# Forget-gate sums added as a spread bias, 64-row score matmuls side by side, and a vector of ones set on the chip

## What is computed

```python
x = x + 0.5 * swiglu(rms_norm(x), ffn1)
p = rms_norm(x) @ w_in        # FoX q, k, v, f; HGRN2 q, f, i, g; S5 u
x = x + concat(fox(p), hgrn2(p), s5(p)) @ w_out
x = x + 0.5 * swiglu(rms_norm(x), ffn2)
```

```python
c = cumsum(log_sigmoid(f_logit), axis=1)            # one row of 256 sums per head
for qs, qe in ((0, 128), (128, 256)):
    s = einsum('bhqd,bhkd->bhqk', q[:, :, qs:qe], k[:, :, :qe]) * scale
    s = s + c[:, :, qs:qe, None] - c[:, :, None, :qe]
    p = softmax(where(mask, s, -inf))
    out = einsum('bhqk,bhkd->bhqd', p, v[:, :, :qe])
```

## Time and profile before

| | |
|---|---|
| median of 3 runs | 1018.65 us (1017.72 to 1018.83) |
| the profiled execution | 1019.28 us |
| its span, first to last instruction | 1017.5 us |
| granted TensorE clock over the span | 1.000 |
| PE busy | 1008.7 us (99%) |
| DVE, ACT, POOL busy | 734.4, 559.8, 225.8 us |
| mean transfer rate | 175 GB/s |

### The profile page before, as it was taken

The page is one execution under the profiler, slowest core; times in us unless marked ns, Lnnn a source line. Parts: engine busy times, 40 slices in busy tenths (PEclk is TensorE's granted clock), DMA queues, the critical chain, the costliest instruction groups (busy, mean ns, idle before and its releaser), DMA issues.

```text
span 1017.5 us, 20399 instructions
## 1 busy us (share of the span) xinstructions
PE 1008.7 (99%) x8434; PEld 941.5 (93%) x8434; DVE 734.4 (72%) x937; ACT 559.8 (55%) x701; POOL 225.8 (22%) x293
## 2 busy tenths in 40 slices
PE   9999999999999999999999999999999999999998
PEld 8898989999999989898999898999999998989898
DVE  5777777889788666666667777777988867565654
ACT  5747453556587645353576555356566865444441
POOL 0004999610002000000020079994000020000000
PEclk9999999999999999999999999999999999999999
DMA  8654545434235454545465454544332355554541
GB/s 304 237 197 164 207 165 206 167 125 147 106 125 207 166 209 164 206 165 206 167 219 213 145 227 150 221 154 174 135 144 104 112 220 190 184 201 170 197 174 42
DMA packets 26817, 178.38 MB, mean 175 GB/s; under 512 B 3120, under 2 KB 4160, under 8 KB 5760
## 3 DMA queue, kind: packets, MB, share of 16 engines
q1 hardware_dynamic: 25056, 172.50, 46.3%
q10 hardware_dynamic: 1584, 4.57, 1.2%
q0 software_dynamic: 112, 0.40, 0.1%
HBM read 176.42 MB, written 1.05 MB: 174 GB/s over the span
## 4 chain that ended last, share of the span: by engine, by line
PE 92%; DVE 3%; DMA 2%; ACT 2%; issue 1%; SPq 0%; POOL 0%; DVEq 0%; ACTq 0%
PE ps L917 24%; PE ps L855 17%; PE ps L856 16%; PE ps L857 16%; PE ps L919 12%; DMA raw<-stream 1%; ACT hi L600 1%; DVE lo L1271 1%; DMA mask<-masks 1%; PE ps L1027 1%; PE ps L1132 1%; DVE in_lo L1490 0%; PE ps L1076 0%; PE ps L1098 0%; SPq L385 0%
## 5 line engine op out<-in xcount | busy, mean ns | idle before, releaser
L917 PE MATMUL ps<-xg,hi 128*128 128x512 f32 x1120 | 397.8, 399 | 0.3
L1271 DVE TENSOR_TENSOR lo<-raw,hi 128x2048 fp32r<-128x2048 f32 x129 | 301.2, 2362 | 132.8 <-ACT hi L600 132.8
L919 PE MATMUL ps<-xg,lo 128*128 128x256 f32 x1120 | 314.5, 281 | 0.0
L600 ACT ACTIVATE hi<-raw 128x2048 fp32r<-128x2048 f32 x129 | 242.6, 1911 | 108.9 <-PE ps L919 81.8
L917 PEld LDWEIGHTS ps<-xg,hi 128*128 128x128 f32 x1120 | 210.5, 188 | 52.0 <-DVE lo L1271 0.9
L919 PEld LDWEIGHTS ps<-xg,lo 128*128 128x128 f32 x1120 | 211.7, 189 | 0.0
L855 PE MATMUL ps<-act_hi,hi 128*128 128x256 f32 x704 | 199.3, 283 | 1.1 <-DVE act_lo L1323 1.1
L856 PE MATMUL ps<-act_lo,hi 128*128 128x256 f32 x704 | 199.2, 283 | 0.0
L857 PE MATMUL ps<-act_hi,lo 128*128 128x256 f32 x704 | 199.1, 283 | 0.0
L855 PEld LDWEIGHTS ps<-act_hi,hi 128*128 128x128 f32 x704 | 134.8, 191 | 3.1 <-issue 1.2
L857 PEld LDWEIGHTS ps<-act_hi,lo 128*128 128x128 f32 x704 | 135.0, 192 | 0.0
(11 more groups left out here) (329 smaller groups left out, 1701.6 us busy)
## 6 DMA issues: line engine op xcount, KB each, us to landing
raw<-stream SPq DMA_DIRECT2D x160, 1024.0 KB, 4.9
par<-params ACTq DMA_DIRECT2D x2, 1463.0 KB, 7.6
raw<-stream SPq DMA_DIRECT2D x8, 256.0 KB, 6.9
rows<-stream SPq DMA_DIRECT2D x2, 1024.0 KB, 7.0
x<-xT ACTq DMA_DIRECT2D x4, 256.0 KB, 6.2
out<-x SPq DMA_DIRECT2D x4, 128.0 KB, 1.9
out<-x ACTq DMA_DIRECT2D x4, 128.0 KB, 2.0
con<-consts POOLq DMA_DIRECT2D x1, 373.5 KB, 6.3
```

Source lines behind the costliest of these rows:

```text
L600: e.activation(hi[slot][:, :], raw[slot][:, :], ACT.Copy).then_inc(hi_written, 1)
L917: pe.matmul(bank(b), hi[slot][:, w:w + P], xg[:, k, :, :].rearrange("p s t -> p (s t)"), start=k == 0, stop=False, skip_group_check=True)
L919: last = pe.matmul(bank(b)[:, 0:T], lo[slot][:, w:w + P], xg_hi[:, k, :], start=False, stop=k == KT - 1, skip_group_check=True)
L1271: v.tensor_tensor(lo[slot][:, :], raw[slot][:, :], hi[slot][:, :].bitcast(F32), ALU.subtract).then_inc(lo_written, 1)
```

## The change

Five edits go together.

1. SP stores the four rows of running sums to a DRAM tensor `cum_rows`, waits for that, and loads them back twice, each time to all 128 partitions, into `gate_bias` (the memory of `w_lag`/`pT`). These three transfers stand in SP's program ahead of the load of unit 8.
2. POOL adds the causal mask into the two diagonal blocks of `gate_bias`; `fox_mask` adds `gate_bias` in place of the mask. The sums now run on the negated logarithms, so that what is added is minus c_s; the c_t of a query is the same for all keys and drops out of the softmax. The six DVE instructions that wrote the extra rows are gone.
3. `fqk` has two heads one above the other on 128 partitions; a score matmul contracts 64 rows, an even head on rows 0 to 63, an odd one on rows 64 to 127.
4. `normalize` writes all 128 partitions in one instruction.
5. The ones are written by a POOL memset and have a semaphore of their own, `ones_set`; `con` is loaded around them in two pieces, and `row_sums` and ACT wait for `ones_set` only. The wait for all constants (now 48) moves to `angles`, `lag_matrix` and POOL's mask addition.

```diff
@@ SP, in the loop over the input units @@
                 for w in range(IN_UNITS):
+                    if w == RING + 5:
+                        sp.wait_ge(cum_ready, l + 1)
+                        sp.dma_start(cum_rows, fl[0:FOX_HEADS, 2, :]).then_inc(cum_stored, 16)
+                        sp.wait_ge(bu_done, l + 1)
+                        sp.wait_ge(cum_stored, l * 16 + 16)
+                        for at, n in ((0, P), (P, T)):
+                            sp.dma_start(gate_bias[:, :, at:at + n],
+                                         cum_rows[:, 0:n].unsqueeze(0).broadcast_to([P, FOX_HEADS, n])
+                                         ).then_inc(cum_spread, 16)
@@ POOL @@
+            pool.memset(ones, 1.0).then_inc(ones_set, 1)
             pool.wait_ge(raw_loaded[2], 16)
-            pool.dma_start(con[:, :], consts).then_inc(consts_loaded, 16)
+            pool.dma_start(con[:, 0:P], consts[:, 0:P]).then_inc(consts_loaded, 16)
+            pool.dma_start(con[:, 2 * P:], consts[:, 2 * P:]).then_inc(consts_loaded, 16)
...
                 sum_squares(l * 3 + 1)
-                pool.memset(fqk[0:64, :, 1:FOX_HEADS:2, :], 0.0).then_inc(heads_cleared, 1)
                 pool.memset(attn[:, :, :], 0.0).then_inc(attn_cleared, 1)
+                pool.wait_ge(consts_loaded, 48)
+                pool.wait_ge(cum_spread, (l + 1) * 32)
+                causal = cmask[:, P:].unsqueeze(1).broadcast_to([P, FOX_HEADS, P])
+                for at in (T, 0):
+                    block = gate_bias[:, :, at:at + P]
+                    pool.tensor_tensor(block, block, causal, ALU.add).then_inc(bias_ready, 1)
@@ ACT, ahead of the layers, and PE, in row_sums @@
-            e.wait_ge(consts_loaded, 32)
+            e.wait_ge(ones_set, 1)
...
-                pe.wait_ge(consts_loaded, 32)
+                pe.wait_ge(ones_set, 1)
@@ PE, fox_scores @@
-                        pe.wait_ge(cum_ready, l + 1)
...
-                    for hd in (2 * pair, 2 * pair + 1):
-                        r = slice(0, GATES if hd % 2 == 0 else P)
-                        last = pe.matmul(bank(6 + hd % 2)[:, pair * n:(pair + 1) * n], fqk[r, 0, hd, tok],
-                                         fqk[r, 1, hd, 0:n], start=True, stop=True, skip_group_check=True)
+                    for odd in range(2):
+                        r = slice(64 * odd, 64 * odd + 64)
+                        last = pe.matmul(bank(6 + odd)[:, pair * n:(pair + 1) * n], fqk[r, 0, pair, tok],
+                                         fqk[r, 1, pair, 0:n], start=True, stop=True, skip_group_check=True)
@@ DVE @@
-                st.mark(v.tensor_tensor(fl[:, 0, :], fl[:, 0, :], fl[:, 1, :], ALU.subtract))
+                st.mark(v.tensor_tensor(fl[:, 0, :], fl[:, 1, :], fl[:, 0, :], ALU.subtract))
...
-                v.wait_ge(heads_cleared, l + 1)
-                for odd in range(2):
-                    r = slice(0, 2 * FOX_HEADS) if odd else slice(64, GATES)
-                    v.tensor_scalar(fqk[r, 0, odd:FOX_HEADS:2, :], cum[r, :].unsqueeze(1).broadcast_to([2 * FOX_HEADS, 2, T]),
-                                    prm("query_rows", 0, 1)[r, :], prm("query_rows", 1, 1)[r, :], ALU.mult, ALU.add)
-                    for hd in (odd, odd + 2):
-                        last = v.tensor_scalar(fqk[r, 1, hd, :], cum[r, :], prm("key_rows", 2 * hd, 1)[r, :],
-                                               prm("key_rows", 2 * hd + 1, 1)[r, :], ALU.mult, ALU.add)
-                last.then_inc(cum_ready, 1)
...
-                    for odd in range(2):
-                        r = slice(64 * odd, 64 * odd + 64)
-                        last = v.scalar_tensor_tensor(fqk[r, w, odd:FOX_HEADS:2, :], plain[r, w, :, :], gain[r, :],
-                                                      fsq[r, w, :].rearrange("p (a t) -> p a t", a=2),
-                                                      ALU.mult, ALU.mult)
-                    last.then_inc(fqk_ready, 1)
+                    v.scalar_tensor_tensor(fqk[:, w, :, :], plain[:, w, :, :], gain,
+                                           fsq[:, w, :].rearrange("p (a t) -> p a t", a=2),
+                                           ALU.mult, ALU.mult).then_inc(fqk_ready, 1)
...
+                    v.wait_ge(bias_ready, l * 2 + 2 - t)
                     for odd in range(2):
                         last = v.tensor_tensor(sc[:, odd:4:2, at:at + n],
                                                bank(6 + odd)[:, 0:2 * n].rearrange("p (h s) -> p h s", h=2),
-                                               cmask[:, 2 * P - n:].unsqueeze(1).broadcast_to([P, 2, n]), ALU.add)
+                                               gate_bias[:, odd:4:2, at:at + n], ALU.add)
```

More of the change, by code:

```diff
@@ L63 @@
                   ("o_gain", HEADS), ("skip", 2), ("glu_b", 2), ("q_gain", 1), ("k_gain", 1), ("f_bias", 1),
-                  ("w_forget", KT * FOX_HEADS), ("query_rows", 2), ("key_rows", 2 * FOX_HEADS), ("b_re", 2 * P), ("b_im", 2 * P),
+                  ("w_forget", KT * FOX_HEADS), ("b_re", 2 * P), ("b_im", 2 * P),
                   ("c_re", S5_TILES * 32), ("c_im", S5_TILES * 32), ("glu_w", 512),
@@ L105, in close @@
         assert self.n == self.per_layer, f"{self.n} steps in a layer, not {self.per_layer}"
-DVE_STEPS = 66
+DVE_STEPS = 65
 POOL_STEPS = 70
@@ L194, in build @@
         fox_mem = ExitStack()
-        fqk = sb("fqk", [P, 2, FOX_HEADS, T], F32, fox_mem)
+        fqk = sb("fqk", [P, 2, 2, T], F32, fox_mem)
+        sb("over_fqk", [P, 4 * T], F32, fox_mem)
         fv = sb("fv", [P, 2, 256], F32, fox_mem)
@@ L215, in build @@
         pT = w_lag[:, :, :, :].rearrange("p a b c -> p (a b c)")
+        gate_bias = pT.rearrange("p (h c) -> p h c", c=384)
+        cum_rows = nc.dram_tensor("cum_rows", (FOX_HEADS, T), F32, kind="Internal").ap()
         fst = sb("fst", [P, 4, 8])
@@ L260, in build @@
         consts_loaded = sem("consts_loaded")
+        ones_set = sem("ones_set")
         x_loaded = [sem(f"x_loaded{q}") for q in range(QUARTERS)]
@@ L340, in build @@
         cum_ready = sem("cum_ready")
-        heads_cleared = sem("heads_cleared")
+        cum_stored = sem("cum_stored")
+        cum_spread = sem("cum_spread")
+        bias_ready = sem("bias_ready")
         sc_done = sem("sc_done")
@@ L1033, in lag_matrix @@
                 def lag_matrix():
+                    pe.wait_ge(consts_loaded, 48)
                     pe.wait_ge(tables_ready, l * 2 + 1)
@@ L1374, in _ @@
             first_sums()
-            v.wait_ge(consts_loaded, 32)
             for l in range(DEPTH):
@@ L1382, in angles @@
                 def angles():
+                    v.wait_ge(consts_loaded, 48)
                     v.wait_ge(par_loaded, l * 16 + 16)
@@ L1637, in _ @@
                 st.wait()
-                st.mark(v.tensor_tensor(fl[:, 0, :], fl[:, 0, :], fl[:, 1, :], ALU.subtract))
+                st.mark(v.tensor_tensor(fl[:, 0, :], fl[:, 1, :], fl[:, 0, :], ALU.subtract))
                 st.wait()
-                st.mark(v.tensor_tensor_scan(fl[:, 2, :], ones[0:GATES, 0:1].broadcast_to([GATES, T]), fl[:, 0, :], 0.0,
-                                             ALU.mult, ALU.add))
+                v.tensor_tensor_scan(fl[:, 2, :], ones[0:GATES, 0:1].broadcast_to([GATES, T]), fl[:, 0, :], 0.0,
+                                     ALU.mult, ALU.add).then_inc(cum_ready, 1)
                 st.mark(v.tensor_scalar(fst[:, 0, 0:1], prm("q_gain"), FOX_DIM ** -0.5, None, ALU.mult))
                 st.wait()
-                cum = fl[:, 2, :]
-                v.wait_ge(heads_cleared, l + 1)
-                for odd in range(2):
-                    r = slice(0, 2 * FOX_HEADS) if odd else slice(64, GATES)
-                    v.tensor_scalar(fqk[r, 0, odd:FOX_HEADS:2, :], cum[r, :].unsqueeze(1).broadcast_to([2 * FOX_HEADS, 2, T]),
-                                    prm("query_rows", 0, 1)[r, :], prm("query_rows", 1, 1)[r, :], ALU.mult, ALU.add)
-                    for hd in (odd, odd + 2):
-                        last = v.tensor_scalar(fqk[r, 1, hd, :], cum[r, :], prm("key_rows", 2 * hd, 1)[r, :],
-                                               prm("key_rows", 2 * hd + 1, 1)[r, :], ALU.mult, ALU.add)
-                last.then_inc(cum_ready, 1)
                 take(5, plain[:, 0, :, :])
@@ L1840, in _params @@
     rows = np.r_[0:2 * FOX_HEADS, 64:GATES]
-    bias, query, key = np.zeros((GATES, 1)), np.zeros((GATES, 2)), np.zeros((GATES, FOX_HEADS, 2))
+    bias = np.zeros((GATES, 1))
     bias[rows, 0] = np.tile(inputs["fox_f_bias"][l], 4)
-    for r in (0, 64):
-        query[r:r + FOX_HEADS, 0] = query[r + FOX_HEADS:r + 2 * FOX_HEADS, 1] = 1.0
-        for hd in range(FOX_HEADS):
-            key[r + hd, hd, 1], key[r + FOX_HEADS + hd, hd, 0] = 1.0, -1.0
     put("f_bias", bias)
-    put("query_rows", query)
-    put("key_rows", key.reshape(GATES, -1))
     forget = inputs["w_in"][l][:, 3 * 256:3 * 256 + FOX_HEADS]
```

## The result

The changed kernel takes 1021.81 us (median of 16 runs, 1019.33 to 1025.44), the kernel before 1018.54 us in the same session (16 runs, 1017.32 to 1019.14): a ratio of 1.0038, 95% interval 1.0029 to 1.0048. It is slower by 3.3 us, above the forecast of 1017.8 us and above the end of its range, 1020.8.

What follows compares the result with a forecast made beforehand. TensorE was taken as the bound, busy for 1008.7 of 1017.5 us. The terms -1.2 (start), -0.1 (scores) and +0.5 (feed) sum to -0.8 us, from 1018.65 to 1017.8 us; range 1015.3 to 1020.8.

Steps and rivals of the forecast that it cites:

- Start: Start of the kernel: without the wait for the masks, ACT's roundings and the down-projection come earlier, about 1.2 us less.
- so it still waits: the gain is ACT's 1.2 us: First down-projection: TensorE arrives earlier but still waits for `act_lo`, so 1.2 us are gained, not the waits' 2.8.
- Scores: TensorE's score matmuls: row pairs cost 0.22 us a layer more, the `normalize` wait goes; 0.1 us less in all.
- Feed: Mix stage: the new transfers delay unit 8 and TensorE ahead of `level(2)`, 0.25 us a layer, about 0.5 us more.
- At the 341 GB/s at which rows of 1 KB were stored 2.3 us: Mix stage: the spread's 786 KB take 2.3 us, or 3.1 if 512 B pieces go at half that rate.
- unit 8 late: Rival, mix stage: spread at half rate takes 4.6 us, TensorE waits 2.2 us a layer, 1021.8 us; chance 0.20.
- The step from the landing to TensorE: Mix stage: no delay up to unit 8 landing at 255.3 us; each microsecond later is one on TensorE.
- loads that follow each other share their lead: Mix stage: reason for taking 0.25 us a layer, in the lower part of 0 to 0.7.

Runs made afterwards that it cites:

- start alone: The kernel before with only the `ones_set` edit (ones by a memset, constants in two pieces, the wait for them moved): 1017.13 us, ratio 0.9998.
- spread behind unit 9: The changed kernel with the store and two spreading loads issued behind unit 9's load, not ahead of unit 8's: 1020.06 us, ratio 1.0014.
- POOL late too: The kernel with the spread behind unit 9, POOL's addition also waiting until DVE has written the last level's keys: 1016.89 us, ratio 0.9988.
- the best order: The changed kernel with the spread behind unit 9, POOL's addition late and eight unused matmuls ahead of the first `act_lo`: 1016.66 us, ratio 0.9986.
- one edit back: The best order with the store and spreading loads put ahead of unit 8 again: 1019.73 us, ratio 1.0014.
- both waits filled: The changed kernel with eight unused matmuls ahead of the first `act_lo` and twelve ahead of `level(2)`: 1019.46 us, ratio 1.0014.

## Why the prediction was wrong

**Start, right in size, with a price left out.** ACT's chain moved up by 1.2 us, unit 4 landed at 24.4 us, TensorE waited 1.9 us (1.5 to 2 forecast). The step that failed is "so it still waits: the gain is ACT's 1.2 us". It turned two waits of 0.8 and 1.1 us, with work between them, into one of 1.9, and gave no price to what comes behind: 3.4 us at half clock, 1.38 us lost in the profiled execution. It doesn't come each time: in the kernels whose mix stage has no wait of over 1.5 us, the clock is below 1.000 in four of eleven runs (start alone), eight of eleven (spread behind unit 9) and two of eleven (POOL late too). Before the change the same 2.8 us of waits were three pieces with work between them, and the clock was 1.000 over the span.

**Scores, right.** Pairs of 0.83 and 0.62 us for 0.81 and 0.60; the wait of 0.24 us for `normalize` is gone. By matching the matmuls of the two traces the scores gave back 0.03 us in the first layer and 0.02 in the second, near the 0.05 a layer of the forecast. Another 0.2 us a layer came further on, at the second transposes of the attention (L1172), where the kernel before waited 0.17 us for `sc` and the changed one doesn't; the forecast has nothing of it. The row before:

```profile
293.65 0.42 PEld L1148 LDWEIGHTS ps<-con,sc 128*128 128x128 f32 x4 [0.17 <-DVE sc L1712]
```

**Feed, the term that failed.** "At the 341 GB/s at which rows of 1 KB were stored 2.3 us": the spread's packets ran from 248.7 to 253.7 us in the first layer, 786 KB in 5.0 us, 157 GB/s. The doubt was written into the rival *unit 8 late*, at half of 341 and 4.6 us, and it had the spread nearly right; rows that a store wrote say nothing of a load that reads the same 4 KB 128 times. Unit 8 landed at 256.5, 0.5 to 1.3 us later than forecast, although the store took 1.3 us and not 1.9. The waits ahead of `level(2)` were 1.3 and 2.2 us in place of 0.2: 1.1 and 2.0 us more, where the forecast had 0.25 a layer. The step from the landing to TensorE held in the first layer: a landing 1.2 us behind the 255.3 us that it gives as harmless, a wait 1.1 us longer. The fall of the clock behind the second wait, 1.45 us, and the late packets of instructions are in no term. The reason given for the low value, that loads that follow each other share their lead, held (the data of unit 8 came within 2.5 us behind the spread) and wasn't enough.

**The sum.** By the ratios, of which 0.001 is 1.02 us: the best order stands 0.0014 below before, the gains, 1.4 us (1.3 forecast); one edit back, the spread ahead of unit 8, is 0.0028 more, 2.9 us; and the changed kernel stands 0.0024 above the one with both waits filled, 2.4 us, the clock. This last kernel and the one with the edit back are both at 1.0014, so the three steps add up to 1.0038; this only divides the result and doesn't test it, and each ratio is known to about 0.0009. The rival's time, 1021.8, is that of the result, but in part by chance: it had 4.4 us for the late unit and nothing for the clock.

The page TensorE: Matmul & The Clock Gate of the Trainium skill gives, in its section HAM oscillation — how this bites in real kernels, the loss of a fall as the time at half clock times one half: an estimate of 1.7 us for 3.4. The traces have 1.38 and 1.45 us, less than this. The medians of the groups of runs lie 1.6 to 2.5 us apart, more than this, but a group with more falls may have longer waits too.

## What to carry to other kernels

Where one engine is busy for 99% of the span, price a wait not by its length alone: removing a wait ahead of another joins the two into a longer one, and a fall of the clock behind it can cost more than the joining saved (1.38 us against 1.16 here). It is cheaper to leave a transfer that nobody needs for 20 us behind the load that is needed next than to be early with it, and a queue's wait for a value stops every load behind it, the engines' programs too, as it seems. An addition on POOL isn't free because POOL is idle: put it where DVE is idle as well.

## What the hardware showed unexpectedly

- Apart from the very end of the execution, the granted clock fell for 3.4 us six times in four profiles, behind waits of 1.7 to 2.2 us; behind waits of 1.5 us and less it fell in none, but neither did it behind three others of 1.7, 2.3 and 2.5 us.
- A DVE subtraction of 128x512 with both inputs in SBUF took 1.73 us and not 0.69 beside an addition on POOL; the four took up to 4.18 us and not 2.49.
- A load that spreads 4 KB of DRAM to 128 partitions in pieces of 512 B and 1 KB moved 157 GB/s.
- The fourteen stalls of TensorE's matmuls without a releaser ended 1.3 to 1.6 us after a 16 KB packet of the instruction queue. With SP's wait ahead of unit 8 that packet ended 1.1 and 1.3 us after `level(2)` had begun, and not 2.0 to 2.8 us ahead of it.
